# Differential attention: the two mask operands kept as 16-bit floats

## The reference, cut to what matters

```
s = einsum('bqhcd,bkhcd->bhcqk', q, k) * (DIFF_DH ** -0.5)
visible = (k_pos // CHUNK)[None, :] <= (q_pos // CHUNK)[:, None]
s = where(visible, s, -1e30)
p = softmax(s, axis=-1)
a = p[:, :, 0] - lam * p[:, :, 1]
o = einsum('bhqk,bkhv->bqhv', a, v)
```

## Time and profile before

| | |
|---|---|
| time, median of 3 runs | 1618.08 us (1616.9 to 1618.85) |
| span of the profiled execution | 1612.1 us |
| what lies around the span, against that median | 6.0 us |
| TensorE busy | 1501.3 us (93%), 7820 instructions |
| VectorE busy | 821.2 us (51%) |
| ScalarE busy | 651.0 us (40%) |
| GpSimd busy | 274.6 us (17%) |
| mask products of the prompt, line 2474 | x128, 10.8 us busy with a mean of 244 ns between 832 and 1110 us |
| mask products of the samples, line 2514 | x32, 7.7 us busy with a mean of 321 ns |

### The profile page before, as it was taken

One profiled execution on the slowest core, in us unless ns is written; L12 is line 12 of the kernel. 1 busy time (PEld: TensorE's weight loads), 2 busy tenths in 40 slices (PEclk: granted clock), 3 DMA queues, 4 the chain that ended last, 5 costly groups with the idle time before them and its releaser, 6 DMA issues.

```text
span 1612.1 us, 21319 instructions
## 1 busy us (share of the span) xinstructions
PE 1501.3 (93%) x7820; PEld 1124.7 (70%) x7820; DVE 821.2 (51%) x1424; ACT 651.0 (40%) x1069; POOL 274.6 (17%) x164
## 2 busy tenths in 40 slices
PE   5999999999999999999999899998999799999981
PEld 3775777577757775778777677776787578877771
DVE  3332341234123412221676767654365699988984
ACT  5322212231223122312445445544223378888871
POOL 1341134113411341133000000000222100000002
PEclk9999999999999999999999999999999699999995
DMA  9524452445244524432441254156630699999985
GB/s 347 154 77 144 154 172 78 144 154 172 78 144 154 171 79 144 144 93 79 161 131 53 79 171 131 46 160 213 204 118 36 233 316 394 394 392 384 387 309 208
DMA packets 158091, 290.31 MB, mean 180 GB/s; under 512 B 15083, under 2 KB 40859, under 8 KB 157733
## 3 DMA queue, kind: packets, MB, share of 16 engines
q1 hardware_dynamic: 154246, 278.47, 50.8%
q0 software_dynamic: 3744, 10.49, 1.8%
HBM read 251.55 MB, written 40.52 MB: 181 GB/s over the span
## 4 chain that ended last, share of the span: by engine, by line
PE 33%; DMA 9%; DVE 4%; issue 3%; ACT 2%; SPq 1%; POOL 0%; DVEq 0%; POOLq 0%; ACTq 0%
PE pj L93 8%; PE pj L95 8%; PE pj L94 8%; DMA m_raw<-w 6%; PE d_B L2472 1%; PE d_B L2491 1%; PE d_B L2499 1%; PE d_B L2533 1%; DMA ring_raw<-w_out 1%; ACT m_hi L1394 1%; DMA ring_raw<-w_br_diff 1%; PE d_B L1569 1%; PE d_B L2481 1%; PE d_B L2460 1%; PE d_B L2510 1%
## 5 line engine op out<-in xcount | busy, mean ns | idle before, releaser
L93 PE MATMUL pj<-ring_hi,hT_hi 128*128 128x512 f32 x880 | 369.5, 420 | 7.5 <-DVE hT_lo L689 3.1
L95 PE MATMUL pj<-ring_hi,hT_lo 128*128 128x512 f32 x880 | 346.2, 393 | 0.0
L94 PE MATMUL pj<-ring_lo,hT_hi 128*128 128x512 f32 x880 | 345.2, 392 | 0.0
L479 POOL TENSOR_TENSOR ring_lo<-ring_raw,ring_hi 128x1024 fp32r<-128x1024 f32 x79 | 190.8, 2416 | 547.2 <-ACT ring_hi L545 547.2
L545 ACT ACTIVATE ring_hi<-ring_raw 128x1024 fp32r<-128x1024 f32 x79 | 83.5, 1059 | 421.8 <-DMA ring_raw<-w_in 357.0
L1473 DVE TENSOR_TENSOR m_lo<-m_raw,m_hi 128x1024 fp32r<-128x1024 f32 x188 | 224.5, 1222 | 24.5 <-ACT m_hi L1394 21.7
L93 PEld LDWEIGHTS pj<-ring_hi,hT_hi 128*128 128x128 f32 x880 | 166.8, 190 | 61.9 <-issue 29.2
L1394 ACT ACTIVATE m_hi<-m_raw 128x1024 fp32r<-128x1024 f32 x188 | 194.4, 1058 | 27.3 <-DMA m_raw<-w 24.2
L95 PEld LDWEIGHTS pj<-ring_hi,hT_lo 128*128 128x128 f32 x880 | 166.1, 189 | 37.0
L94 PEld LDWEIGHTS pj<-ring_lo,hT_hi 128*128 128x128 f32 x880 | 167.2, 190 | 28.6 <-issue 1.0
L736 DVE SCALAR_TENSOR_TENSOR r_S<-r_S,g,r_sm 128x512 f32<-128x512 f32 x64 | 45.3, 745 | 123.6 <-PE r_sm L986 123.6
(11 more groups left out here) (342 smaller groups left out, 2352.8 us busy)
## 6 DMA issues: line engine op xcount, KB each, us to landing
m_raw<-w SPq DMA_DIRECT2D x188, 512.0 KB, 10.8
ring_raw<-w_in SPq DMA_DIRECT2D x72, 512.0 KB, 3.8
r_S<-state_ret SPq DMA_DIRECT2D x64, 256.0 KB, 4.6
r_ada_raw<-w_ada SPq DMA_DIRECT2D x16, 1024.0 KB, 6.8
o_state_s<-r_S SPq DMA_DIRECT2D x64, 256.0 KB, 4.7
a_raw<-w_ada SPq DMA_DIRECT2D x8, 1024.0 KB, 12.2
ring_raw<-w_in SPq DMA_DIRECT2D x32, 256.0 KB, 3.2
ring_raw<-w_br_ret SPq DMA_DIRECT2D x16, 512.0 KB, 4.1
```

The costliest lines, as they stand in the source:

```text
L93: pe.matmul(out, s_hi, m_hi, start=start, stop=False)
L94: pe.matmul(out, s_hi, m_lo, start=False, stop=False)
L95: return pe.matmul(out, s_lo, m_hi, start=False, stop=stop)
L479: pool.tensor_tensor(lo[:, p], raw[:, p], hi[:, p].bitcast(F32), ALU.subtract).then_inc(lo_done, 1)
```

## The change

The tiles `mp` and `ms` that TensorE reads become bfloat16 (16-bit floats). The transfers bring the float32 constants into two new tiles, `mp_in` and `ms_in`, and GpSimd converts them at the start of `phase_d`, after its two memsets; each conversion raises the new semaphore `mask_set`. TensorE's `scores` waits for `mask_set` in place of `mask_in`. The new tiles lie where `qT` and `kT` of half 0 are written later, so ScalarE waits for `mask_set` before its first copy into `qT` (`take_T(0, 0, 0)`). The allocator reserves four bytes for an element of any type, so no other tile moves. In `scores` and `s_scores` the calls themselves are unchanged; with 16-bit operands each mask product is one instruction.

```diff
-        mp = sb("d_mask_p", [P, P + CHUNK], F32)
-        ms = sb("d_mask_s", [P, 3 * P], F32)
+        mp = sb("d_mask_p", [P, P + CHUNK], BF16)
+        ms = sb("d_mask_s", [P, 3 * P], BF16)
...
+        sb = Map(nc, at + 20480, at + 24576)
+        mp_in = sb("d_mask_p_in", [P, P + CHUNK], F32)
+        ms_in = sb("d_mask_s_in", [P, 3 * P], F32)
...
-        rope_in, lam_in, mask_in = map(sem, ("rope_in", "lambda_in", "masks_in"))
+        rope_in, lam_in, mask_in, mask_set = map(sem, ("rope_in", "lambda_in", "masks_in", "masks_set"))
...
-            sp.dma_start(mp[:], io["mask_p"]).then_inc(mask_in, 16)
-            sp.dma_start(ms[:], io["mask_s"]).then_inc(mask_in, 16)
+            sp.dma_start(mp_in[:], io["mask_p"]).then_inc(mask_in, 16)
+            sp.dma_start(ms_in[:], io["mask_s"]).then_inc(mask_in, 16)
...
+            pool.wait_ge(mask_in, 2 * 16)
+            pool.tensor_copy(mp[:], mp_in[:]).then_inc(mask_set, 1)
+            pool.tensor_copy(ms[:], ms_in[:]).then_inc(mask_set, 1)
...
             def take_T(i, a, t):
                 job_done(act, "T", i, a, t)
+                if i + a + t == 0:
+                    act.wait_ge(mask_set, 2)
...
             def scores(i, u):
                 t, h, nk = unit_of(u)
-                pe.wait_ge(mask_in, 2 * 16)
+                pe.wait_ge(mask_set, 2)
```

## The result

In four runs beside four of the kernel before, the changed kernel took 1607.01 us (median; 1605.16 to 1608.92) against 1617.80 (1616.90 to 1618.85): a ratio of 0.9936, with a 95% interval of 0.9922 to 0.9949. Two later groups of runs gave 0.9933 (0.9913 to 0.9953) and 0.9962 (0.9948 to 0.9976). Over all runs of the study the mean is 1607.5 us for the changed kernel (19 runs, standard error 0.41) and 1615.9 for the one before (48 runs, 0.38; 1610.5 to 1625.1), so the change is worth 8.4 us, give or take 1.1 (twice the error of the difference, 0.56).

The account below looks back on a forecast made before the run. TensorE was taken to bound the attention, except from 876 to 912 us, where VectorE has its highest share. Prompt 3.2 plus samples 2.1 make 5.3 us, so 1618.1 becomes 1612.8 us, range 1610.5 to 1617.3.

Parts of the forecast that it names:

- The prompt units: Prompt mask products on TensorE: one instruction less saves 0.135 us a unit, 24 paid units, 3.2 us.
- case A: Rest before the next load counted from the last pass's recorded start: only 2.9 us gained, 1615.2 us; chance 0.18.
- where the array changes between a part of its rows and all of them: Where TensorE's rest of about 0.10 us before the next load was said to come.
- The sample streams: Sample mask products on TensorE: 0.16 us saved a stream with the load kept at 0.11, 13 streams, 2.1 us.
- Rival B: 16-bit mask load in the streams takes 0.03 us, not 0.11: 1.0 us more gain, 1611.8 us; chance 0.12.
- The count of 13 paid streams: Sample streams on the chain whose saving counts, leaving out those ending in waits for keys (921, 951, 1060 us).
- The conversions: GpSimd's two mask conversions at the start end by 781, before ScalarE's first wait at 795.8: cost 0.
- Rival C: Gain absorbed by VectorE already late before 876 and by key transfers: 2.0 us left, 1616.1 us; chance 0.15.
- Rival D: Number format change empties the array before prompt mask products, 0.46 us each: 5.7 us slower, 1623.8 us; chance 0.08.
- The number 1612.8: Whole kernel: span 1612.1 us plus 6.0 around it, 1618.1, the median of the runs, less 5.3.
- The low end of the range: 1610.5 us: Rival B with all eight other prompt units also paid.
- So the gain is carried to the end: After the attention, output projection, router and experts start from TensorE's own progress, so the gain is kept whole.

Follow-up runs that it names:

- a: The changed 16-bit kernel again with no edit, against the kernel before: 1607.06 us (six runs), ratio 0.9933.
- b: The changed kernel with new tiles, conversions and semaphore but masks kept float32, against the kernel before: 1615.89 us, ratio 1.0002.
- i: The kernel before, unedited, run once more with a trace: 1613.23 us.
- k: The kernel before, unedited, run another time with a trace: 1617.05 us.
- h: The changed kernel with both mask products left out, so nothing is masked, against the kernel before: 1606.88 us, ratio 0.9948.
- e: The changed kernel with masks in float32r (one pass, four bytes) in place of 16-bit, against the kernel before: 1607.22 us, ratio 0.9952.
- c: The changed kernel with only the prompt masks in 16 bits, sample masks float32, against the kernel before: 1612.41 us, ratio 0.9972.
- d: The changed kernel with only the sample masks in 16 bits, prompt masks float32, against the kernel before: 1615.03 us, ratio 0.9984.
- f: The 16-bit kernel with the sample mask's stationary operand cut from 128 to 96 columns: 1606.85 us (one run).
- l: The changed 16-bit kernel, unedited, run once more with a trace: 1608.85 us.

## Why the prediction was right and wrong

*The prompt units: right.* The block shrank by 0.13 to 0.14 us, as worked out from the end of the columns and not from the recorded start, so case A is refuted. Between execution a and before the distances of the mask products' starts shrink by 0.13 to 0.15 us for each unit from the first to the eleventh (the fourth by 0.49, of which 0.35 is a wait that the first trace of before and b had and i and k had not), by 0.00 from the twelfth to the sixteenth (VectorE's stretch, as read from the earlier trace rows), and in the second half by 0.13 to 0.16 for all but two units. In sum 3.4 us without the 0.35, against 3.2. That the rest comes "where the array changes between a part of its rows and all of them" is too narrow: in h it stands behind sample scores that use all 128 rows and 32 columns.

*The sample streams: the step that failed.* "I take the high end, since every load of 128 columns here has it": the load of 0.11 us was kept for 16-bit masks, and so the term of the streams was mis-sized, 13 x 0.16 = 2.1 us. Measured were 0.256 us a stream in place of 0.16 (0.413 to 0.157 us from load to load). The difference of 0.10 is the load, as e shows, which has the long load and 0.25 us. Rival B was right about the mechanism, and still a little short of the size: it put the load at 0.03 us, and 0.157 - 0.053 - 0.09 leaves about 0.01. The count of 13 paid streams nearly held in a against before: the distance behind the stream at 921 shrinks by 0.03 only and the one behind 951 grows by 0.31, both ahead of a wait for keys as foreseen, and all others inside a half shrink by 0.23 to 0.28, the one at 1060 among them. In sum the samples bring 3.4 us in place of 2.1, 3.1 of them inside the attention; with 3.4 of the prompt and the 0.35 that makes the 6.9.

*The conversions: right.* 0, by b, as far as its runs can tell.

*Rival C: in part.* The waits for keys took 3.2 us in place of 1.0 in the first trace, 1.9 to 3.9 in the others, where b had 0.9, i and k 1.7 and 2.4. Most of that is a gain that a stream can't pass on, and some of it more: in the first 16-bit trace the distances behind the streams at 932, 951 and 1060 grew by 0.13 to 0.51 us, because the keys came later than before and not only no earlier. VectorE was not late before 876. In the traces with a low clock stretch something is given back by the clock and not by VectorE's queue (1.4 to 1.6 us by the later one); I had no rival for that, and the prediction had put the clock at nothing.

*Rival D: refuted.* 16-bit products follow float32 ones with no restart between; the 0.35 us ahead of the scores is unchanged.

*The number 1612.8.* Against the measured 1607.0, it misses by 5.8 us. The first part, 2.2 us, is the starting point: the median of three runs was 1618.1, the mean of 48 is 1615.9. The trace gave the sign of it: its span of 1612.1 us left 6.0 to the median, and I filed that under "around the span" where all 41 later runs of before have 1.8 to 1.9; the rest was the spread of the executions. Among these 41 the nine with a mean clock above 0.9725 took 1612.9 us on average and the 15 at 0.9705 or below 1618.0, so much of the spread goes with the clock. The median of the four runs of the changed kernel lies 0.5 below the mean of 19. What is left is a gain of 8.4 us where 5.3 was forecast, 3.1 too much; some 1.3 us of it (13 x 0.10) is the samples' load. The low end of the range, by its own terms 1611.8 - 8 x 0.135, is 1610.7 and not 1610.5, which changes nothing here.

*What comes after the attention.* "So the gain is carried to the end" put nothing on what follows. The traces show a further 1.8 us there (514.8 to 513.0, four against five traces, each group spread over 3 us). It lies ahead of the experts. From the last sample score to the first product of the experts (`m_hi`) it is 177.1 to 180.3 us in eight traces: the three of before, b, c, d, a and h. It is 174.5 to 176.5 in six: the other four of the 16-bit kernel, e and f. Behind that point the 16-bit kernel has no gain (337.1 against 336.8 us on average). In the eight TensorE waits 2.9 to 4.3 us near 1165 us and a low clock stretch follows; in the six the longest distance between products there is 1.5 us and the clock stays.

The same six differ from the same eight some 35 us earlier, by one transfer, the last piece of `w_br_diff`. It lands 5.0 to 5.2 us after its issue in the six and 3.6 to 3.8 in the eight. The DMA view of the first 16-bit trace from 1128.5 to 1134 us, and what TensorE then waits for,

```profile
q1 hardware_dynamic: 272, 0.52, 31.8%
q8 instruction: 1, 0.02, 1.1%
ring_raw<-w_br_diff SPq DMA_DIRECT2D x1, 512.0 KB, 5.2
...
PE pj L93 <- DVE ring_lo L2283: 1.4, 1, 1.4
```

and that of before from 1132.8 to 1138 us, with TensorE's wait between 1160 and 1180:

```profile
q1 hardware_dynamic: 272, 0.52, 32.9%
ring_raw<-w_br_diff SPq DMA_DIRECT2D x1, 512.0 KB, 3.8
...
PE d_B L2599 <- DVE g_mT_lo L2346: 3.0, 1, 3.0
```

The queue `q8 instruction` brings the program's own instructions, 16 KB a packet. In each of the six such a packet begins 2.5 to 3.1 us behind the issue of the piece. In a it begins 3.3 us behind, when the piece's own packets are nearly through, and in the other seven none lies in the transfer. Where it lies goes with the kernel: 38 to 40 us behind the last sample score in the 16-bit kernel, e and f, which have the same number of TensorE instructions, 50 to 52 in before and b, 33, 59 and 58 in c, d and h. So fewer instructions moved the packet into the transfer. TensorE then waits for the piece, by distances of 1.6 to 1.8 us between products, comes later to the place near 1165 and finds less to wait for.

That fits the parts c and d adding up to less than the whole, and h gaining less time than its attention does: all three lack the late piece. But no run moved the packet alone, so of this chain the coincidence in all fourteen traces is shown, and the cause is argued. Packets of the same queue may lengthen waits for keys too (the three longest, 1.4 to 1.5 us in d, k and l, each follow a transfer of 5.2 to 5.6 us with such a packet 2.7 to 3.3 us behind its issue), but four other key transfers took as long without one.

*What stays open.* Of the 8.4 us in the runs the traces hold 7.0, 5.2 in the attention and 1.8 behind it. The remaining 1.4 is little more than the 1.1 by which the 8.4 is uncertain, and no trace locates it. Why the clock fell behind 890 us in some executions and not in others is not shown either.

## What to carry to other kernels

A small constant operand in float32 costs more than its size suggests on a busy TensorE: a second pass, a second weight load, and a load that isn't the fast one. Where a load stands uncovered, as in the sample streams here, its own duration is on the path, and the format decides it (0.10 of 0.26 us); where it is hidden behind a product, as in the prompt units, only the pass counts (0.14 us with 16 bits and float32r alike). A wait 70 us behind the changed code can go with a change of the number of instructions, so what follows is not simply carried along. And before a change of half a percent is forecast, the spread of the executions has to be known: a span that lies far below the median is a message about it.

## What was not expected of the hardware

A weight load of 96 columns in 16 bits is neither the fast one nor the one of four-byte values: its block is 0.182 us, against 0.157 for 128 columns in 16 bits and 0.252 for 128 columns of float32r. By 0.05 us of columns and 0.09 of rest it takes about 0.04 us, half of what 96 columns would take at the four-byte pace of 0.84 ns each.

The rest of about 0.09 us between the last column and the next load, where the used part of the array changes, appears with float32, float32r and 16-bit operands alike. It appears without a mask product too: in h, behind sample scores of 128 rows and 32 columns, 0.20 us lie between the last product's start and the next load, of which its 128 columns take 0.11.

The same wait of 3.06 us in the same kernel was followed by the lower clock in one execution and not in another (0.57 and 1.00 in the rows above). A stretch at the lower clock cost nothing near 895 us, where VectorE sets the pace, and 1.4 to 1.6 us near 983 or 1039, where TensorE does.

One packet of 16 KB with the program's instructions goes with a transfer of 512 KB landing 1.3 us later, 5.1 in place of 3.8 us, in six traces of six; begun 3.3 us behind the issue instead of 2.5 to 3.1, as in a, it left the landing at 3.8.
